# Full attentions of a hybrid encoder: probabilities scaled by GpSimd before they are transposed, outputs kept by channel, three buffers of probabilities

## The reference

```python
def dense_attention(q, k, v):
    ...
    def attend(q_blk):
        logits = jnp.einsum("bqkgd,bskd->bkgqs", q_blk, k).astype(jnp.float32) * scale
        p = jax.nn.softmax(logits, axis=-1).astype(v.dtype)
        return jnp.einsum("bkgqs,bskd->bqkgd", p, v)
...
y = jnp.concatenate([y_a, y_b, y_c, y_d], axis=-1) * jax.nn.silu(gate_path)
branch = jnp.einsum("bsnc,ncd->bsnd", y.reshape(b, s, N_BRANCH, BRANCH_W), w_branch[l])
gates = jax.nn.sigmoid(merge_logits.reshape(b, s, N_BRANCH, D_MODEL))
x = x + jnp.sum(gates * branch, axis=2) @ w_out[l]
```

## Time and profile before

| | |
|---|---|
| three runs, median (lowest to highest) | 2740.06 us (2738.78 to 2741.49) |
| the profiled execution, own time | 2739.07 us |
| its span | 2737.3 us |
| TensorE busy | 2652.6 us, 97% |
| VectorE, ScalarE, GpSimd busy | 1286.7, 1007.7, 775.5 us |
| mean granted TensorE clock | 0.996 |

### The profile page before, as it was taken

How to read it: one execution, slowest core, us unless ns; L and a number is a source line. 1 busy time by engine, 2 the same in 40 slices (tenths; PEclk the granted TensorE clock), 3 DMA queues, 4 the chain that set the end, 5 groups by cost and what they waited for, 6 DMA issues and landing times.

```text
span 2737.3 us, 36490 instructions
## 1 busy us (share of the span) xinstructions
PE 2652.6 (97%) x13956; PEld 2236.1 (82%) x13956; DVE 1286.7 (47%) x2668; ACT 1007.7 (37%) x2074; POOL 775.5 (28%) x534
## 2 busy tenths in 40 slices
PE   6999999999999999999999999999999999999998
PEld 4788878878888888878897887888888888888787
DVE  3575265722344355542346734675224443555323
ACT  3364114711344534521225631165124445354111
POOL 2310341024243342123422114200334342322232
PEclk9999999999999999999999999999999999999999
DMA  5100211011111231111420002100211213211122
GB/s 183 32 9 2 57 43 32 1 53 41 47 46 43 67 91 47 31 39 43 158 69 22 1 23 54 37 20 1 65 44 44 54 42 82 76 39 30 49 100 93
DMA packets 200376, 137.52 MB, mean 50 GB/s; under 512 B 20952, under 2 KB 186456, under 8 KB 200168
## 3 DMA queue, kind: packets, MB, share of 16 engines
q1 hardware_dynamic: 186380, 128.69, 16.6%
q10 hardware_dynamic: 13824, 6.49, 0.8%
HBM read 120.24 MB, written 19.10 MB: 51 GB/s over the span
## 4 chain that ended last, share of the span: by engine, by line
PE 90%; DVE 5%; ACT 2%; issue 1%; POOL 1%; DMA 0%; ACTq 0%; SPq 0%; POOLq 0%; DVEq 0%
PE ps L925 24%; PE ps L888 10%; PE ps L890 10%; PE ps L889 10%; PE ps L1126 4%; PE ps L1092 4%; PE ps L1076 4%; PE ps L988 3%; PE ps L990 3%; PE ps L989 3%; PE ps L1050 3%; PE ps L1051 3%; PE ps L1061 2%; PE ps L1053 1%; PE ps L1364 1%
## 5 line engine op out<-in xcount | busy, mean ns | idle before, releaser
L2199 POOL CAST wh<-wraw 128x1024 fp32r<-128x1024 f32 (+2 forms) x152 | 169.3, 1114 | 1625.7 <-PE ps L890 788.6
L888 PE MATMUL ps<-xh,wh 128*128 128x512 f32 x1088 | 426.7, 392 | 2.2 <-ACT pt_split L1630 2.2
L890 PE MATMUL ps<-xh,wl 128*128 128x512 f32 x1088 | 423.7, 389 | 0.0
L889 PE MATMUL ps<-xl,wh 128*128 128x512 f32 x1088 | 423.4, 389 | 0.0
L2201 POOL TENSOR_TENSOR wl<-wraw,wh 128x1024 fp32r<-128x1024 f32 (+2 forms) x152 | 401.0, 2638 | 12.2
L925 PE MATMUL ps<-xh,wh 128*128 128x512 f32 x896 | 366.4, 409 | 3.2 <-ACT att L1445 1.2
L925 PE MATMUL ps<-xh,wl 128*128 128x512 f32 x896 | 357.2, 399 | 0.0
L925 PE MATMUL ps<-xl,wh 128*128 128x512 f32 x896 | 356.4, 398 | 0.0
L1477 ACT ACTIVATE gs<-ps 128x512 f32<-128x512 f32 x96 | 57.0, 598 | 519.2 <-PE ps L890 514.7
L888 PEld LDWEIGHTS ps<-xh,wh 128*128 128x128 f32 x1088 | 204.3, 188 | 44.2 <-ACT pt_split L1630 3.0
L890 PEld LDWEIGHTS ps<-xh,wl 128*128 128x128 f32 x1088 | 204.2, 188 | 43.0
(11 more groups left out here) (279 smaller groups left out, 5057.9 us busy)
## 6 DMA issues: line engine op xcount, KB each, us to landing
wraw<-in_w_in_dram SPq DMA_DIRECT2D x128, 512.0 KB, 3.9
acc<-in_x_dram SPq DMA_DIRECT2D x16, 512.0 KB, 8.5
wraw<-in_w_branch_dram SPq DMA_DIRECT2D x64, 128.0 KB, 4.0
wraw<-in_w_out_dram SPq DMA_DIRECT2D x16, 512.0 KB, 3.5
dil_out<-cst ACTq DMA_DIRECT2D x96, 66.0 KB, 1.6
toep<-toep_row SPq DMA_DIRECT2D x16, 256.0 KB, 6.0
xres<-acc SPq DMA_DIRECT2D x8, 512.0 KB, 2.6
acc<-xres SPq DMA_DIRECT2D x8, 512.0 KB, 6.9
```

The costliest lines, as they stand in the source:

```text
L888: pe.matmul(dst, ah, bh, start=i == 0, stop=False)
L889: pe.matmul(dst, ah, bl, start=False, stop=False)
L890: last = pe.matmul(dst, al, bh, start=False, stop=i == len(ks) - 1)
L2199: inc(pool.tensor_copy(high, raw), w_hi[l])
```

## The change

The softmax's division moves from the outputs to the probabilities. VectorE makes the reciprocal of a unit's sum as soon as its exp is done (`sum_inverse`), GpSimd multiplies the 128x1024 probabilities by it in place (`dense_rows`), and TensorE transposes the scaled ones. So the value product, with 64 channels by 256 queries for the high part and the same for the rest, needs no scaling by query afterwards: it stays by channel. The fold's matmuls, the output transposes and the constant `fold` go. ScalarE copies one half of the product (the one of the partitions that the head does not have in `gs`) to `pair_other`, VectorE adds the other half from PSUM (`pair_added`), and GpSimd multiplies the sum onto the gates `gs` in place; for the pairs of the last two tiles VectorE does that itself.

Transposes and value products move one step back (units s-3 and s-2, values of s-4), and the loop is one step shorter at its end. The probabilities get a third buffer, the place of the table `rope_b`, which is therefore loaded in each layer after A's last transposes and not at the start. B's pairs become one head for two tiles, as in A. The second token tile of B and the first two merge tiles of B are split by GpSimd in parts, one part a step, and the queries of A inside the same loop. Several semaphores are merged.

```diff
+        prob_ring = [prob[:, 0, :], prob[:, 1, :], rope_b[:, :, :, :].rearrange("p t a c -> p (t a c)")]
...
-                u["o"] = ps[:, 6 + s // 2 % 2, (s % 2 + 4) * HD:(s % 2 + 5) * HD]
+                u["prob"] = prob_ring[s % 3]
...
         def plan_dense(b):
-            y = []
-            for s, begun, paired, tiles_of in dense_steps(b):
-                y += [tgroup("dve") for _ in tiles_of(s - 6)]
-                for part, x in ((1, s - 2), (0, s - 1)):
+            for s, begun, paired in dense_steps(b):
+                for part, x in ((1, s - 3), (0, s - 2)):
                     if begun(x):
                         units[x]["groups"].append((tgroup("dve"), units[x]["chunks"][4 * part:4 * part + 4]))
-            return y
+            return []
+
+        def product_rows(pair):
+            h = units[2 * pair]["head"] % 2
+            return slice(h * HD, (h + 1) * HD), slice((1 - h) * HD, (2 - h) * HD)
+
+        def product_places(pair):
+            u = units[2 * pair]
+            own, c, t0 = product_rows(pair)[0], u["head"] // 2, u["st"] * P
+            if pair_units(pair)[0] == 2 * pair:
+                return [(gs[own, c, t0:t0 + 2 * P], slice(0, 2 * P))]
+            return [(gs[own, c, t0 + e * P:t0 + (e + 1) * P], slice((1 - e) * P, (2 - e) * P)) for e in range(2)]
+
+        def gated_last(pair):
+            return units[2 * pair]["st"] == ST - 2
...
# SyncE
+                for t in branches[0]["gate_tiles"] + branches[1]["tok_tiles"]:
+                    load_tile(t)
+                sp.wait_ge(t_ready[l], units[branches[0]["span"][1] - 1]["groups"][-1][0] + 1)
+                load(rope_b[:, :, :, :], c_rope_b.rearrange("(t p) a c -> p t a c", p=P), rope_b_in)
+                for t in branches[0]["merge_tiles"] + branches[1]["gate_tiles"] + branches[1]["merge_tiles"]:
+                    load_tile(t)
...
# TensorE
                 def transposes_part(s, part):
-                    pe.wait_ge(exp_done[l], s + 1)
+                    pe.wait_ge(rows_scaled[l], s + 1)
...
-                        for st in tiles_of(s - 6):
-                            pe.wait_ge(o_freed_dve[l], units[s - 6]["o_count"])
-                            y_transposes(next(y), yn[:, st % 2, :])
                         if begun(s):
...
                             logits(s)
+                        if begun(s - 3):
+                            transposes_part(s - 3, 1)
                         if paired(s - 4):
-                            pair = (s - 4) // 2
-                            pe.wait_ge(pair_emptied[l], pair + 1)
-                            for e, v in enumerate(pair_units(pair)):
-                                inc(pe.matmul(units[v]["o"], pair_out[:, pair % 2, e * P:(e + 1) * P],
-                                              fold[:, :], start=True, stop=True), pv_done[l])
-                        if begun(s - 2):
-                            transposes_part(s - 2, 1)
-                        if paired(s - 3):
-                            u = units[s - 3]
+                            u = units[s - 4]
...
-                        if begun(s - 1):
-                            transposes_part(s - 1, 0)
+                        if begun(s - 2):
+                            transposes_part(s - 2, 0)
...
# ScalarE
                             if begun(s - 1):
                                 exps(s - 1, u0)
-                            if begun(s - 2):
-                                high_part(s - 2, 1)
+                            if begun(s - 3):
+                                high_part(s - 3, 1)
...
-                                inc(act.activation(pair_out[:, pair % 2, :], units[s - 3]["product"], ACT.Copy),
-                                    pair_emptied[l])
+                                inc(act.activation(pair_other[own, pair % 2, :], units[s - 4]["product"][other, :],
+                                                   ACT.Copy), pair_emptied[l])
-                            if begun(s - 1):
-                                high_part(s - 1, 0)
+                            if begun(s - 2):
+                                high_part(s - 2, 0)
...
# VectorE
+                def sum_inverse(s):
+                    c = s % U_MAX
+                    dve.wait_ge(exp_done[l], s + 1)
+                    inc(dve.reciprocal(rs[:, c:c + 1], ssum[:, c:c + 1]), sums_set[l])
+
+                def pair_added(pair):
+                    own = product_rows(pair)[0]
+                    dve.wait_ge(pair_emptied[l], pair + 1)
+                    if pair >= 2:
+                        dve.wait_ge(pair_gated[l], pair - 1)
+                    inc(dve.tensor_tensor(yn[own, pair % 2, :], units[2 * pair]["product"][own, :],
+                                          pair_other[own, pair % 2, :], ALU.add), o_freed_dve[l], 2)
+                    if gated_last(pair):
+                        dve.wait_ge(o_freed_dve[l], units[2 * pair + 1]["o_count"])
+                        dve.wait_ge(pair_gated[l], pair)
+                        for dst, cols in product_places(pair):
+                            ins = dve.tensor_tensor(dst, dst, yn[own, pair % 2, cols], ALU.mult)
+                        inc(ins, pair_gated[l])
...
                         if begun(s):
                             maxima(s, u0)
+                        if begun(s - 1):
+                            sum_inverse(s - 1)
                         if paired(s - 5):
-                            pair_outputs(s - 6)
+                            pair_added((s - 5) // 2)
+                        if begun(s - 3):
+                            rest_part(s - 3, 1)
                         if begun(s - 2):
-                            rest_part(s - 2, 1)
-                        if begun(s - 1):
-                            rest_part(s - 1, 0)
+                            rest_part(s - 2, 0)
...
# GpSimd
+                def dense_rows(b, weights):
+                    for s, begun, paired in dense_steps(b):
+                        if b["n"] == 0 and paired(s) and s // 2 + A_RING < 2 * ST:
+                            queries(s // 2 + A_RING)
+                        if begun(s - 1):
+                            x, c = s - 1, (s - 1) % U_MAX
+                            pool.wait_ge(sums_set[l], x + 1)
+                            inc(pool.tensor_scalar(units[x]["prob"], units[x]["prob"], rs[:, c:c + 1], None, ALU.mult),
+                                rows_scaled[l])
+                        if paired(s - 5) and not gated_last((s - 5) // 2):
+                            pair = (s - 5) // 2
+                            own = product_rows(pair)[0]
+                            pool.wait_ge(o_freed_dve[l], units[s - 5]["o_count"])
+                            pool.wait_ge(rows_scaled[l], min(s, b["span"][1]))
+                            for dst, cols in product_places(pair):
+                                ins = pool.tensor_tensor(dst, dst, yn[own, pair % 2, cols], ALU.mult)
+                            inc(ins, pair_gated[l])
+                            pool.wait_ge(pair_gated[l], pair + 1)
+                        if s - b["span"][0] >= 3:
+                            next(weights, None)
...
+                    if t == tok_b[1]:
+                        dense_rows(branches[0], split_steps(t, 2))
+                    elif t == merge_b[0]:
+                        dense_rows(branches[1], itertools.chain(split_steps(t, 5), split_steps(t + 1, 5)))
```

More of the change, by code:

```diff
@@ L16 @@
 from contextlib import ExitStack
+import itertools
 import numpy as np
@@ L447, in build @@
                 u0 = len(units)
[L448 to L453, removed]
+                for st, h in ((a + c, b) for a in range(0, ST, 2) for b in range(HEADS) for c in range(2)):
+                    kv = h // 2
+                    unit(bq_stack[:, h, st * P:(st + 1) * P], bk_stack[:, kv, 0, :], None,
+                         plain_chunks(lambda j: vb[j][:, kv, :]), "dve", st=st, head=h,
+                         k_rest=bk_stack[:, kv, 1, :])
                 b["passes"].append(dict(tiles=t, units=(u0, len(units))))
@@ L788, in _ @@
                             load_tile(tok_a[1])
-                    load(rope_b[:, :, :, :], c_rope_b.rearrange("(t p) a c -> p t a c", p=P), rope_b_in)
-                    sp.wait_ge(toep_masked, 1)
+                    sp.wait_ge(setup_done, MASKED_ROWS)
                     load(toep_row.rearrange("(k h) o -> h k o", k=4), toep_rows[:, :, :], toep_stored)
@@ L1309, in _ @@
                     pe.wait_ge(exp_done[l], b["passes"][-1]["units"][1])
-                    last_y = b["y"][-1]
+                    last_y = b["y"][-1] if n == 3 else units[u1 - 1]["groups"][-1][0]
                     pe.wait_ge(t_freed_dve[l], tgroups[last_y][1])
@@ L1409, in exps @@
                         src = u["logits"]
-                        if s - 2 >= u0:
-                            act.wait_ge(t_ready[l], units[s - 2]["groups"][-1][0] + 1)
+                        if s - 3 >= u0:
```

(22 more changed lines are left out.)

111 lines of the change are left out of this document (47 added, 64 removed).

## The result

The change made the kernel slower: 2812.47 us median (2810.55 to 2814.02) against 2739.73 on the same chip, ratio 1.0264, 95% interval 1.0247 to 1.0282. The forecast was 2719, the range 2690 to 2737. It is rival 3, GpSimd as the bound, and it cost more than that rival said.

What follows compares the result with a forecast made beforehand. TensorE, busy 97% of the span, was taken as the bound. Two layers, each 9.2 us less in A and 1 after B, gave -20 against 2739.07: 2719 us, range 2690 to 2737.

Steps and rivals of the forecast that it cites:

- rival 3: GpSimd becomes the bound: 2740 at 2.4 us a scaling, over 2760 at 3.0; chance 0.12.
- the price of the scaling: GpSimd's 128x1024 scaling per unit, taken as 1.1 to 1.3 us between bounds of 1.07 and 2.46.
- the sum: GpSimd's work per pair, some 4.4 us in A and 5.5 in B, said to fit inside both periods.
- the rest of the sum: Forecast apart from the scaling's price: A 9.2 us shorter, B's stage no gain, about 1 us won after it, per layer.
- The removed work: On TensorE in A and B: folds 25 us, output transposes 6 us, besides their waits.
- The new round: VectorE's reciprocal and pair_added delay the bank T1 needs: pairs of 6.78 us in A, 6.63 in B.
- Rival 4: GpSimd's scaling blocks VectorE's rest_part and pair_added: 0.9 us a pair, 47 in all, 2766; chance 0.04.
- Its formula: GpSimd work per pair at 2.4 us a scaling: 7.0 in A, 5.8 in B, 8.0 there with weight steps.
- its own sum: Lateness at 2.4 us a scaling: 0.25 x 13 in A, 1.3 x 5 + 0.1 x 8 in B, 21 us in all.
- Its threshold: Scaling duration on GpSimd from which it was said to decide the kernel's time: 2.3 us.

Runs made afterwards that it cites:

- k1: Changed kernel with GpSimd scaling only 384 of each unit's 1024 columns: 2730.39 us, ratio 0.9964.
- k11: Changed kernel with a plain GpSimd copy of the 1024 columns onto themselves in place of the scaling: 2729.21 us, one run.
- k9: Changed kernel with the queries split behind the step's scaling on GpSimd instead of ahead of it: 2800.74 us, ratio 1.022.
- k5: Changed kernel with the scaling as tensor_tensor by a broadcast column and pair_added behind rest_part on VectorE: 2732.61 us, ratio 0.9979.
- k8: Changed kernel with the scaling by the constant 1.0 instead of a column of sums: 2803.96 us, one run.
- k4: Changed kernel with GpSimd scaling only 704 of each unit's 1024 columns: 2751.88 us, ratio 1.0045.
- k6: k5 with the queries split behind the scaling on GpSimd instead of ahead of it: 2723.98 us, ratio 0.994.
- k10: k6 with the weight-split steps taken only in every other step: 2718.11 us, ratio 0.9917.
- k12: k10 with the changed kernel's tensor_scalar scaling put back, its three changes of order kept: 2793.13 us, ratio 1.0194.

## Why the prediction was wrong

**The step that failed** is the price of the scaling: "It reads one tensor, so I take 1.1 to 1.3", between a cast of 1.07 and a subtraction of 2.46. It measured 2.845, above both ends. Neither row was of the kind of the new instruction. Number of inputs was the wrong way to sort it: with one tensor and a constant 2.77, with two operands 1.90. The Trainium skill (GPSIMD Engine Reference, Engine selection) has one-input operations at roughly line rate and two-input ones about twice slower; the copy agrees with the first half (1.04 us for 1024 columns), this `tensor_scalar` does not. For two inputs, VectorE's `rest_part` takes 0.69 us for 512 columns, so 1.38 for 1024; GpSimd's product took 1.4 times that and its subtraction 1.8 times. Here the two-operand product is faster than the one-operand one. That the sum should stand by this rule gave the step a support that it didn't have.

**The forecast with that term right.** k1 and k11 have the scaling at 1.25 and 1.04 us and come to 2730 and 2729. So the rest of the sum was 11 us too low and still inside the range. By stages: A 120.2 for 116.5, B 131.9 for 129.4, together 12 in two layers. Nearly half of that are the pairs: A 6.89 on average (6.78 forecast), B 6.73 (6.63), because every other pair is 0.27 longer, with a wait for the bank of 0.82 in B instead of 0.55; 0.21 over 13 pairs of each make 2.7 a layer. The rest lies at the ends of the stages; its source stays open.

**The removed work** was sized rightly: 31 us of TensorE forecast, 30.0 between the busy times of before and k1 (2652.6 and 2622.6). **The new round** was read rightly: reciprocal and `pair_added` ahead of `rest_part(s,1)` make a pair of A 6.89 where TensorE's own work takes 6.43, a wait of 0.46 (0.33 forecast); moved behind it, 23 us come free. **Rival 4** is refuted: `rest_part` took up to 0.693 beside a GpSimd that was working 85% of the stretch.

**Rival 3** had the right mechanism and too small a price. Its formula gives pairs of 7.8 in A and 8.9 in B with weight steps at a scaling of 2.845; measured in k9 7.8, and in the changed kernel 9.0. Put through its own sum, that is 13 x 1.0 in A and 5 x 2.3 in B, some 25 us a layer, 2770. In the first layer the stages lost 47.9 against the forecast (146.6 - 116.5 and 147.2 - 129.4). The other 23 have these sources. They overlap, so this is an account and no exact split: in A they come to 19 where 17 is missing, in B 4 of 6 stay without one.

- 6 are the remainder that k1 shows too (3.7 in A, 2.5 in B).
- 8.5 are the difference of A between the changed kernel and k9, with the same work on every engine. There the granted clock is 0.86 and 0.98. Over the whole run TensorE's busy time for the same 13636 instructions is 2653.1 in the changed kernel, 2637.3 in k9, 2622.6 in k1. That the clock is the way is argued from these rows, since no edit changed the clock alone. Executions of one and the same kernel bear it out: k5's nine reach from 2730.64 us, with a mean granted clock of 0.995, to 2738.75 with 0.989, and in k8 the first layer's A, up to the start of the fourth early token product, took 138.7 us at a granted clock of 0.94 and the second's 142.8 at 0.92. The uneven pairs (GpSimd idle 1.49 us in front of every fourth scaling or so, for a sum that TensorE's slowed logits delayed) fit it.
- 7 are A's start. From A's first logits to its first values it is 17.3 us in k9 (to 154.44) and 13.2 in k1 (to 149.82), with longer first scalings and some 4 us at the lower clock; the second values come 10.7 us later and not the 7.8 of the later pairs, since the two weight steps of A (1.9 us each) stand in front of scalings there. Rival 3 counted the weight steps in B and forgot those in A.

**Its threshold** of 2.3 us for a scaling fell with k4: at 2.05 us TensorE waited 34 us for GpSimd, and 8 in k1. The formula sets GpSimd's sum against the pair; but scalings are wanted one by one, and one that stands behind 1.9 us of gating and queries, or of gating and a weight step, is late long before the sum is full. k6 and k10 show it from the other side: with the same work at 1.90 us, two changes of order give 14 us.

**The chances.** The upper bound of the price should have held cases above the nearest row. No row showed the operation; the forecast, which took the price from the cheaper of two rows, had 0.55 and the whole of rival 3 0.12.

## What to carry to other kernels

Price a new instruction by a row of its own kind, or leave the price open upwards: copy, `tensor_scalar` and `tensor_tensor` over the same 128x1024 elements on the same engine differed by a factor of 2.7 here, and neither the number of inputs nor the place told the order. When work goes to an idle engine, add up that engine's instructions for one period (when it is full, this sets the pace, as in A of k9 and k12, which differ in order and not in time), and then list what stands ahead of each result that someone waits for. An idle TensorE could cost twice here: the wait, and behind some waits the matmuls at the lower clock.

## What the runs showed of the hardware

- GpSimd's multiplication of 128x1024 fp32 in place: as `tensor_scalar` by a column 2.845 us, by a constant 2.77; as `tensor_tensor` with a broadcast column 1.895; copy 1.04. `tensor_scalar` at 384, 704 and 1024 columns: 1.246, 2.047, 2.845.
- `tensor_scalar` by a column kept its duration, 2.835 to 2.857 us in 128 instructions, beside a VectorE at work; and VectorE's `rest_part`, with one operand in PSUM, kept its own, 0.659 to 0.693 in 256, beside GpSimd.
- In the changed kernel, after waits of 1.84 us (at 200.29) and 2.97 (at 502.07), 512-column matmuls started 0.43 us apart for a few us, and not 0.23; the four transposes behind the wait of 2.97 lasted 1.12 us, not 0.60. Not each such wait did it, and shorter ones did: behind one of 1.80 in B (at 493.09) and one of 2.29 in k9's A (at 162.88) the logits kept their 0.23, and behind one of 1.49 at the start of k9's A (at 144.49) they did not. Ahead of A's first logits TensorE is idle for 1.56 to 1.64 us in all of them: in the kernel before and in k1 the logits behind it started 0.23 apart, in the changed kernel they went over to 0.43 some 1.7 us later. From 150 to 250 us k9 waited 1.1 to 1.3 us in most pairs at a granted clock of 1.00.
